# Sample tokens ahead of tile 7 in the out-projection, and the first expert's gate and up weights split during attention

## The reference

```python
h = rmsnorm(x, norm1); z = h @ w_in            # gated linear attention + differential attention
mix = concat(gla_out, diff_out)                # (tokens, 1024)
x = x + mix @ w_out                            # the out-projection
h2 = rmsnorm(x, norm2)
lg = h2 @ w_rg + b_rg                          # router: 4 groups
le = h2 @ w_re[g] + b_re[g]                    # 4 experts in the chosen group, top 2
hid = silu(h2 @ w_gate[e]) * (h2 @ w_up[e])    # 16 experts, d=1024, ff=256
x = x + sum_e gate_e * (hid @ w_down[e])
y = rmsnorm(x, norm_f)
```

## Time and profile before

| what | value |
|---|---|
| median of 3 runs | 915.57 us (909.41 to 921.23) |
| the profiled execution | 914.89 us, of which the span on the core is 913.1 us |
| mean granted TensorE clock | 0.943 of full |
| busy: PE, DVE, ACT, POOL | 788.1, 561.8, 444.9, 249.2 us |
| DMA | 154.70 MB, mean 169 GB/s |

### The profile page before, as it was taken

How to read it: one execution, slowest core, us unless ns; L and a number is a source line. 1 busy time by engine, 2 the same in 40 slices (tenths; PEclk the granted TensorE clock), 3 DMA queues, 4 the chain that set the end, 5 groups by cost and what they waited for, 6 DMA issues and landing times. The chain is left out here.

```text
span 913.1 us, 16430 instructions
## 1 busy us (share of the span) xinstructions
PE 788.1 (86%) x6255; PEld 494.6 (54%) x6255; DVE 561.8 (62%) x921; ACT 444.9 (49%) x855; POOL 249.2 (27%) x170
## 2 busy tenths in 40 slices
PE   3999979959899989976999998882389999998785
PEld 2766634335546644423566665441277787676551
DVE  6643569775444632248688875245675677787748
ACT  5432012557662412236467675234435757777733
POOL 2112987721134000002001000000424453532204
PEclk8999989979999999997999999986579999999998
DMA  9415795501031368881011101153596989999864
GB/s 310 102 50 151 234 300 183 194 0 47 1 99 47 93 224 256 258 279 69 25 70 70 71 24 47 47 209 129 190 312 222 293 259 302 304 338 342 233 207 186
DMA packets 98691, 154.70 MB, mean 169 GB/s; under 512 B 13573, under 2 KB 63301, under 8 KB 98610
## 3 DMA queue, kind: packets, MB, share of 16 engines
q1 hardware_dynamic: 91266, 132.97, 43.8%
q0 software_dynamic: 5728, 16.94, 7.3%
q10 hardware_dynamic: 1616, 3.70, 1.1%
HBM read 128.97 MB, written 27.48 MB: 171 GB/s over the span
## 5 line engine op out<-in xcount | busy, mean ns | idle before, releaser
L912 POOL TENSOR_TENSOR kv<-kv,gt 128x1024 f32<-128x1024 f32 x32 | 80.6, 2540 | 50.3 <-DMA kv<-in_cache_k 50.2
L2329 PE MATMUL ps<-hT_reg,w_reg 128*128 128x344 f16 x288 | 90.1, 313 | 3.5 <-DVE hT_reg L1564 3.5
L2330 PE MATMUL ps<-hT_reg,w_reg 128*128 128x344 f16 x288 | 89.9, 312 | 0.0
L2331 PE MATMUL ps<-hT_reg,w_reg 128*128 128x344 f16 x288 | 89.9, 312 | 0.0
L940 POOL TENSOR_TENSOR rst<-rst,neghalf 128x1 f32<-128x1 f32 (+3 forms) x27 | 24.8, 918 | 225.9 <-DVE rst L1861 225.9
L980 POOL DMA_INDIRECT sum_scratch<-kv,dest x23 | 59.4, 2583 | 89.9 <-DMA sum_scratch<-kv,dest 78.3
L2329 PE MATMUL ps<-w_reg,hT_reg 128*128 128x512 f16 x192 | 73.1, 381 | 1.9 <-ACT kv L1161 1.9
L2330 PE MATMUL ps<-w_reg,hT_reg 128*128 128x512 f16 x192 | 73.0, 380 | 0.0
L2331 PE MATMUL ps<-w_reg,hT_reg 128*128 128x512 f16 x192 | 72.9, 380 | 0.0
L1880 DVE TENSOR_REDUCE mxs<-ps 128x1 f32<-128x640 f32 (+7 forms) x48 | 45.7, 952 | 29.9 <-PE ps L2688 29.8
L2329 PE MATMUL ps<-hT_reg,dg_reg 128*128 128x128 f16 (+5 forms) x256 | 54.1, 238 | 2.0 <-DVE hT_reg L2157 2.0
(11 more groups left out here) (429 smaller groups left out, 2085.6 us busy)
## 6 DMA issues: line engine op xcount, KB each, us to landing
kv<-in_cache_k SPq DMA_DIRECT2D x64, 256.0 KB, 3.4
w_reg<-in_w_gate SPq DMA_DIRECT2D x16, 1024.0 KB
w_reg<-in_w_up SPq DMA_DIRECT2D x16, 1024.0 KB
w_reg<-in_w_down SPq DMA_DIRECT2D x16, 1024.0 KB, 14.8
w_reg<-in_w_in SPq DMA_DIRECT2D x12, 1024.0 KB, 6.6
mix_reg<-in_cache_v SPq DMA_DIRECT2D x32, 256.0 KB, 3.0
kv<-in_cache_v SPq DMA_DIRECT2D x32, 256.0 KB, 3.0
mix_reg<-in_x_prompt SPq DMA_DIRECT2D x8, 512.0 KB, 8.5
```

The lines of the kernel that those rows point to most:

```text
L912: pool.tensor_tensor(pg, pg, qbc[:, b % 2].unsqueeze(1).to_broadcast([P, 2, 512]), ALU.mult).then_inc(s_kq, 1)
L2329: pe.matmul(out, lh, rh, start=start, stop=False)
L2330: pe.matmul(out, lh, rl, start=False, stop=False)
L2331: return pe.matmul(out, ll, rh, start=False, stop=stop)
```

## The change

1. The order of the late tiles becomes 6, 8, 7 (`LATE`); on all engines `p` is a position and `LATE[p]` the tile. The sample tokens' transposes, partial products, copies and sum move into the attention loop's tail (`u` from `UN + 6` to `UN + 9`), in other banks, and ahead of tile 7's product.
2. `w_gate` and then `w_up` of expert 0 are loaded one after the other into the second quarter of the staging (`mst[0][:, 2048:4096]`), which the early `h2` tiles do not use: `w_gate` early in attention, `w_up` once DVE's low part of `w_gate` is written. ACT and DVE split them at `UN + 3`/`UN + 6` and `UN + 4`/`UN + 7`.
3. `product(6)` is cut in two halves of 24 matmuls: one between tile 4's high and low transposes, one behind the low ones. The two halves of the sample's partial products stand around tile 5's low transposes. Tile 7's product is cut in halves too, with tile 6's transposes between them.
4. For tile 7, now last, the high part's transposes wait for the high part alone, DVE reads the low transposes while ACT reads the high ones, and DVE's mean is issued apart from the wait for the root.

```diff
+LATE = (*range(EARLY + 1), NT, NT - 1)
...
+            sp.wait_ge(s_wol, KC // 2)
+            load("w_gate", 1, expert(0), 0, s_mw)
             for t in range(EARLY):
...
+                if t == EARLY - 1:
+                    sp.wait_ge(s_mlo, 1)
+                    load("w_up", 1, expert(0), 0, s_mw)
...
-            for t in range(EARLY, EARLY + 2):
-                sp.dma_start(xr[:, t % 2], x_p[t]).then_inc(s_xr[t % 2], 16)
-            for i in range(2):
-                sp.wait_ge(s_h2o[i], 16 * (EARLY // 2))
-            sp.wait_ge(s_h2T, 2 * EARLY)
-            load_gate_up(0)
...
+            sp.dma_start(xr[:, 0], x_p[EARLY]).then_inc(s_xr[0], 16)
+            sp.dma_start(xr[0:NB, 1], x_s).then_inc(s_xr[1], 16)
...
+                if u == UN + 3:
+                    split_first(0)
+                if u == UN + 6:
+                    act.wait_ge(s_mT, MIXED + NT + 1)
+                    act.activation(mixh[:, 4:8, SEQ:T], ps[:, 6, 0:4 * NB].rearrange("p (k b) -> p k b", k=4),
+                                   ACT.Copy).then_inc(s_mh, 1)
+                    split_first(1)
+                if u == UN + 8:
+                    x1_square(EARLY, x1[:, EARLY])
+                if u == UN + 9:
+                    act.wait_ge(s_sp, PARTS["out"])
+                    act.activation(gt[:, 0], ps[:, 2, :], ACT.Copy).then_inc(s_spe, 1)
...
+            h2_hi(EARLY)
+            x1_square(EARLY + 1, x1[0:NB, NT])
+            h2_hi(EARLY + 1)
+            read_late(EARLY)
+            read_late(EARLY + 1)
+            x1_square(NT, x1[:, NT - 1])
+            h2_hi(NT)
+            act.wait_ge(s_h2T, EARLY + NT + 1)
+            act.wait_ge(s_rt, NT - 1)
+            act.activation(h2T[:, NT % 2, 0], bank16(4).rearrange("p (k t) -> p k t", k=KC), ACT.Copy).then_inc(s_hTh, 1)
...
+                if u == UN + 7:
+                    dve.wait_ge(s_mh, MIXED + NT + 1)
+                    dve.tensor_tensor(mixl[:, 4:8, SEQ:T], ps[:, 6, 0:4 * NB].rearrange("p (k b) -> p k b", k=4),
+                                      mixh[:, 4:8, SEQ:T], ALU.subtract).then_inc(s_ml, 1)
+                    add_x(EARLY)
+                if u == UN + 9:
+                    dve.wait_ge(s_sp, PARTS["out"] + 1)
+                    dve.wait_ge(s_spe, PARTS["out"])
+                    dve.tensor_copy(gt[:, 1], ps[:, 3, :]).then_inc(s_spe, 1)
...
+                if u in (UN + 4, UN + 7):
+                    split_first((u - UN) // 7)
...
+            norm_x1(NT)
+            logits(EARLY, 6)
+            scale_x1(NT)
+            h2_lo(NT)
+            logits(EARLY + 1, 6)
+            dve.wait_ge(s_h2T, EARLY + NT + 2)
+            dve.wait_ge(s_rt, NT - 1)
+            dve.tensor_copy(h2T[:, NT % 2, 1], bank16(5).rearrange("p (k t) -> p k t", k=KC)).then_inc(s_hTh, 1)
+            logits(NT, 6)
...
+                if u == UN + 4:
+                    product(EARLY, 0)
+                if u == UN + 8:
+                    product_part(0)
                 if u % H == 0 and 0 <= (u - 20) // H < EARLY:
                     early_transpose((u - 20) // H, 1)
+                if u == UN + 8:
+                    product_part(1)
                 if u % H == 1 and 0 <= (u - 21) // H < EARLY:
                     early_router((u - 21) // H)
                 if u == UN + 4:
-                    product(EARLY)
...
+                    product(EARLY, 1)
+                if u == UN + 6:
                     pe.wait_ge(s_dec, DEC["normed"])
...
+                if u == UN + 9:
                     product_sum()
...
+            product(NT, 0)
+            late_transpose(EARLY)
+            product(NT, 1)
+            late_transpose(EARLY + 1)
+            late_router(EARLY)
+            late_router(EARLY + 1)
+            late_transpose(NT, True)
+            late_router(NT, 2)
```

More of the change, by code:

```diff
@@ L591, in hidden_before, with first_parts @@
             return e - 1 if one_bank(e) and one_bank(e - 1) else e
+        def first_parts(lo):
+            return [(egl, eul)[j][0] if lo else (egh, euh)[j][0] for j in range(2)], \
+                mst[0][:, 2048:4096].rearrange("p (k f) -> p k f", k=KC), [egh[0], euh[0]]
         def expert_parts(s, lo):
@@ new lines, in _ @@
+            norm_x1(EARLY)
+            scale_x1(EARLY)
+            h2_lo(EARLY)
+            add_x(EARLY + 1)
+            norm_x1(EARLY + 1)
+            scale_x1(EARLY + 1)
+            h2_lo(EARLY + 1)
+            dve.wait_ge(s_x1o, 16 * EARLY)
+            dve.tensor_scalar(iom, iof[:, 0:4], -64.0, None, ALU.add)
+            dve.tensor_scalar(iof_p, iof[:], SCL, None, ALU.mult)
+            dve.tensor_scalar(iof_c, iof[:, 0:COLS], P * SCL, None, ALU.mult)
+            for c in range(2):
+                dve.tensor_scalar(r_tv[:, 9 * c:9 * c + 9], tokid[:], 1.0, None, ALU.add)
@@ L2583, in attn_transpose, with product @@
                 ins.then_inc(s_mT, 1)
-            def product(t):
-                r = rows(t)
-                pe.wait_ge(s_wol, KC // 2)
+            def product(p, half):
+                t = LATE[p]
                 pe.wait_ge(s_ml, MIXED + t + 1)
                 pe.wait_ge(s_p, 2 * UN)
-                if t >= 2:
-                    pe.wait_ge(s_x1, 2 * (t - 1))
-                for half in range(2):
-                    cs = slice(512 * half, 512 * half + 512)
-                    for k in range(KC):
-                        ins = split_mm(ps[0:r, 2 * (t % 2) + half, :], mixh[:, k, span(t)], mixl[:, k, span(t)],
-                                       wo_hl[k // 4][0][:, k % 4, cs], wo_hl[k // 4][1][:, k % 4, cs], k == 0,
-                                       k == KC - 1)
-                    ins.then_inc(s_om, 1)
@@ new lines, in product, with product_part @@
+                for k in range(KC):
+                    ins = split_mm(ps[:, 2 * (p % 2) + half, :], mixh[:, k, span(t)], mixl[:, k, span(t)],
+                                   wo_hl[k // 4][0][:, k % 4, cs], wo_hl[k // 4][1][:, k % 4, cs], k == 0, k == KC - 1)
+                ins.then_inc(s_om, 1)
+            def product_part(half):
+                pe.wait_ge(s_ml, MIXED + NT + 1)
+                cs = slice(512 * half, 512 * half + 512)
+                sample_parts(2 + half, mixh, mixl, lambda k: wo_hl[k // 4][0][:, k % 4, cs],
+                             lambda k: wo_hl[k // 4][1][:, k % 4, cs])
@@ L2752, in _, with late_transpose @@
-                if t == NT - 1:
-                    product_parts()
-                if t >= EARLY + 2:
-                    v = t - 2
-                    r = rows(v)
-                    pe.wait_ge(s_rtr, v)
-                    pe.wait_ge(s_hTh, 2 * EARLY + v + 1 - EARLY)
-                    for k in range(KC):
-                        ins = split_mm(ps[0:r, 6, 0:NG + NE], h2T[:, v % 2, 0, k, 0:r], h2T[:, v % 2, 1, k, 0:r],
-                                       wrh[:, k], wrl[:, k], k == 0, k == KC - 1)
-                    ins.then_inc(s_rt, 1)
+            def late_transpose(p, apart=False):
+                r = rows(LATE[p])
+                pe.wait_ge(s_h2h, p + 1)
+                if not apart:
+                    pe.wait_ge(s_h2l, p + 1)
+                if p > EARLY:
+                    pe.wait_ge(s_hTh, EARLY + p)
+                else:
+                    bank4_free()
+                    pe.wait_ge(s_x1, 2 * EARLY)
+                for lo in range(2):
+                    if apart and lo:
+                        ins.then_inc(s_h2T, 1)
+                        pe.wait_ge(s_h2l, p + 1)
+                    for k in range(KC):
+                        ins = pe.transpose(bank16(4 + lo)[:, r * k:r * k + r],
+                                           h2s[0:r, p % 2, D * lo + P * k:D * lo + P * k + P], ident16[0:r, 0:r])
+                ins.then_inc(s_h2T, 1)
@@ new lines, in late_router @@
+            def late_router(p, reads=1):
+                r = rows(LATE[p])
+                pe.wait_ge(s_rtr, p)
+                pe.wait_ge(s_hTh, EARLY + p + reads)
+                for k in range(KC):
+                    ins = split_mm(ps[0:r, 6, 0:NG + NE], h2T[:, p % 2, 0, k, 0:r], h2T[:, p % 2, 1, k, 0:r],
+                                   wrh[:, k], wrl[:, k], k == 0, k == KC - 1)
+                ins.then_inc(s_rt, 1)
+            product(NT, 0)
+            late_transpose(EARLY)
+            product(NT, 1)
```

195 lines of the change are left out of this document (74 added, 121 removed).

## The result

The changed kernel takes 903.41 us, the median of 4 runs (901.22 to 907.13). The kernel before took 914.59 beside it (4 runs, 909.41 to 921.23). The ratio is 0.9868 with a 95% interval of 0.983 to 0.9906, so the change saves between 8.6 and 15.5 us: faster, and within 2%.

What follows compares the result with a forecast made beforehand. It took the stage between attention and the experts, where PE idles, to be the bound. Its steps moved the last logits from 634.35 to 622.8, 11.5 us earlier, the rest shifting along: median 915.57 to 904, range 897 to 911.

Steps and rivals of the forecast that it cites:

- Product 6 in the gap: PE behind tile 4's high transposes: half of product 6 fills 2.70 us of idle and avoids the low clock, gain 4.3 us.
- Tile 5's low part and the load of x: Behind tile 4's logits: low part at 588.9, load of tile 6's x issued about 590.5, landing 3.5 us later at 594.0.
- The sample's sums: Behind tile 6's addition: the two sums on PE take 1.9 us, done at 600.0, when tile 7's product starts.
- Product 7: On PE from 600.0, starting at the low clock: 13.2 us plus tile 6's transposes (0.9), to 614.1, covering the sample's chain.
- The last tile: From tile 7's second-half addition, done at 614.8, to the last logits at 622.8, 11.5 us earlier than before.
- The rest moves too: SP's queue ahead of the experts: `w_up(1)` 4.0 us late behind tile 7's rows, covered by ACT's 5.38 idle, cost nothing.
- given back ahead of the experts: Ahead of the experts: `w_up(1)` lands later and meets the gather, 3 to 6 us lost, about 908.5; chance 0.20.
- The clock stays up: Product 7 on PE needs 11.3 us at full clock, 2.6 us more gained, gain of 14, 901.5; chance 0.12.
- The load of x holds everything: DVE's wait for tile 6's x delays ACT and PE; landing 15 us after issue, the gain is gone; slower, chance 0.05.
- No effect: The logits end earlier, but the experts' stage keeps its own pace from a fixed-work resource: 915 us; chance 0.05.

Runs made afterwards that it cites:

- clock kept: Changed kernel with 16 matmuls of zeros, on a bank nothing reads, put into PE's 3.52 us wait: stage 48.2 us, ratio 0.9863 to the kernel before.
- the best version: Changed kernel with x for tile 6 and the samples loaded ahead of SP's wait for w_gate's low part: stage 44.8 us twice, ratios 0.9823 and 0.981.
- the weights alone: Kernel before with only the early load and split of the first expert's weights: stage 60.8 us, ratio 1.0017.

## Why the prediction was right, and where a term was off

The time (904.0 predicted, 903.41 measured), its side and the mechanism were right. That the totals agree within 0.6 is partly luck: the interval of the ratio is 7 us wide, the changed kernel repeated has 905.26, and the stage, which can be told better, gave 10.0 and not 11.5. By its own steps, with 3.08 taken off the times of after:

1. *Product 6 in the gap: right.* No wait, clock 1.00 from 577 to 585; tile 7's attention transposes at 588.4, predicted 588.7. The first half ends at 585.28 (582.2), the cover of 0.7 us was enough. The transposes come 4.5 us earlier than before (592.97), where the step said 4.3; that is parting and the weight split in ACT's stream together.
2. *Tile 5's low part and the load of x: right but for the load.* Low part at 588.7 (588.9), issue at 590.4 (590.5), addition at 594.85 instead of 594.0. The load took 4.39 us behind the 512 KB write, where 3.5 was taken.
3. *The sample's sums: this is the term that was mis-sized.* The prices from the earlier trace rows (1.02 us each) are of sums at full clock. The step itself leaves PE waiting ahead of the sums, and behind the wait of 3.52 us they cost 1.87 and 1.91: 3.6 together instead of 1.9. With the load's 0.9, product 7 starts at 602.7 instead of 600.0. The low clock was seen in the next step and priced there, one step too late. The two experiments on it show it from both sides: with x early and with the clock kept, the sums take 1.02 each.
4. *Product 7: gives 1.9 of these 2.7 back.* It was to run its first part at the low clock as before, 14.1 us with tile 6's transposes; part of that stretch had now passed with the sums. Window 605 to 612 shows 0.84 (1.1 us lost, 1.9 assumed), and its end is at 614.9, predicted 614.1. The sample's chain ended at 610.7 (610.4) and was covered, as said.
5. *The last tile: 0.7 longer.* 9.4 us from the last addition to the logits instead of 8.7. The low part's 8 transposes took 1.04 at the low clock (0.5 taken), the same mistake in small. The logits come at 624.3, predicted 622.8. Of the parts of this step only the low part's was tried alone: 2.1 us.
6. *The rest moves too: right.* `w_up(1)` landed 12.36 us behind the last logits (639.78 - 627.42), before 10.73: 1.6 late, where 4.0 was forecast, and ACT kept 4.44 us of idle (1.4 forecast). The price was 2.9 us, for 1 MB in the queue. In the rows most of the 1.6 is lost ahead of the loads' issue: from the first issue of the group (the tile's rows) to that of `w_down(0)` it takes 2.1 us instead of 1.0 before (631.28 to 632.30), mainly as the issue of the zeros ahead of it takes 1.17 us; from there `w_down(0)` lands after 7.3 us, before 6.8. The Trainium skill, "DMA: Bandwidth & Descriptors", section "Queues, rings and completion order", says that each DMA engine takes a ring's descriptors in order, which puts the weights behind the rows. `w_down(0)` is only 0.5 us longer under way than before, so no run here shows more than a remainder of them ahead of it; whether the long issues come from the same 1 MB, the runs don't tell.

The rivals: *given back ahead of the experts* did not come. The first expert matmul is 27.4 us behind the logits (26.7 before), but over all fourteen profiled executions this is 26.7 to 28.2 without a pattern, so 0.7 can't be given to the change; and with the loads moved ahead nothing is gained. *The clock stays up* did not come by itself, but the run with the clock kept shows what it would have been: 48.2, a gain of 12.6 of the 14 that it promised. *The load of x holds everything* named the right place in the stream; the load took 4.39 us and not 15. But the wait it leaves is what the best version removes, and the prediction looked at it only as a risk. *No effect* is out.

One thing speaks for the price taken at step 3: in the earlier trace rows the sums stand behind a wait too, of 3.11 us, and PE's granted clock was still 1.00. The window of the kernel before, columns as in the earlier trace rows:

```profile
620.00:622.00 2.00, 1.88 (x4) 0.26 (x4) 1.37 (x2) 1.87 (x2) 0.00 (x0) 1.00 0.00 0
```

So a wait of about 3 us does not always bring the clock down; with the weights alone, behind 2.83 us, the same sums took 1.16 and 1.91.

The Trainium skill, "TensorE: Matmul & The Clock Gate", Part 1, says that the low clock is the default and that activity releases it. The rows of this kernel agree: the same pair of matmuls takes 1.87 us behind the wait and 1.02 where the wait is filled or gone. Taken up at step 3 instead of in a rival, the low clock would have given the sums 3.6 us as one of two cases; the sums of the earlier trace rows, at full clock behind 3.11 us, are the other.

The prediction opens with the 9.91 us transfer in the chain of before. It never priced it by itself, and rightly built its sum from the engines' steps: moved alone, the transfer gives nothing.

What stays open: executions differ by some microseconds ahead of the stage. The one edit that acts there is the early load of `w_gate`, and no cost of it shows: the stage starts at 570.6 to 577.7 in the eleven executions with it and at 573.5 to 577.2 in the three without. And product 7 ends 0.9 to 1.2 us earlier in two executions, in which no edit touches it. The clock comes back sooner there, inside the second pair of sums; PE's timeline of the kernel with the low part not apart:

```profile
596.98 1.87 PE L2644 MATMUL ps<-gt,sel 128*8 128x512 f32 x2
598.65 1.42 PE L2646 MATMUL ps<-gt,sel 128*8 128x512 f32 x2
```

The second pair takes 1.42 where after has 1.91 (with the expert loads first, 1.41; with product 6 whole, 1.74, and there too product 7 is done 0.9 us sooner behind the sums' start). Why it comes back at another moment, the runs don't tell.

## What to carry to other kernels

Price each instruction at the clock that the new schedule gives it: if a step leaves PE waiting, what stands behind the wait may cost nearly twice its price in a busy stretch (here 1.87 and 1.91 us for 1.02), and removing a wait can pay more than its length (6.0 us for waits of 4.50 and of 3.52). Since a wait of 3.11 us in the kernel before left the clock full, carry both prices. A transfer in the chain that ended last is worth only what no other engine does beside it: the weights' move gave nothing in the old order, 3.0 us in the new one and 3.9 with product 6 parted too. When a wait for a load is what is left, look first at where its issue stands in the queue and when its memory is really free: four moved lines made the stage 6.0 us shorter.

## What the runs showed of the hardware

- A pair of f32 matmuls of 128x512 takes 1.02 us at the full clock and 1.87 to 1.91 at the low one.
- PE's wait of 3.52 us in the changed kernel ends in a window (599 to 605) with a granted clock of 0.62, and it is 0.50, the lower of the two levels (1.2 GHz), from 601 to 605 with PE busy again. With 16 matmuls of zeros in that wait the clock was 1.00. In the kernel before, a wait of 3.11 us left it at 1.00.
- Most DMA issues on SP around the stage take 0.3 to 0.7 us; in the group behind tile 7's rows some take 1.17, 1.43 and 1.49.
- A 512 KB load issued 0.42 us behind a 512 KB write landed after 4.39 us, against 3.2 on a quiet queue.
